# A position-bias table read in reversed query order, and softmax factors applied to the attention outputs

## The reference, cut to what matters

```python
def attend(qg, k, v):                                   # branch 1: grouped-query attention
    s = einsum('bqhgd,bkhd->bhgqk', qg, k) * ATTN_SCALE
    p = softmax(s, axis=-1)
    return einsum('bhgqk,bkhd->bqhgd', p, v)

# branch 2: neighbourhood attention on an 8 x 64 grid of tokens, window 8 rows x 16 columns
    s_win = einsum('bqhd,bwqjhd->bhqwj', q_row, k_win) * ATTN_SCALE
    row_bias_idx = r0 + arange(wr) - r + (NA_WIN_ROWS - 1)
    bias = rpb[:, row_bias_idx][:, :, col_bias_idx]      # rpb: 8 heads x 15 x 31
    s_win = s_win + bias
    s_ctx = einsum('bqhd,bkhd->bhqk', q_row, k_ctx) * ATTN_SCALE
    p = softmax(concatenate([s_win, s_ctx]), axis=-1)
    out = p_win @ v_win + p_ctx @ v_ctx
```

## Time and profile before

| | |
|---|---|
| median of 3 runs | 2911.68 us (2910.14 to 2912.68) |
| profiled execution, its own time | 2918.17 us |
| its span (first to last instruction) | 2916.4 us |
| mean granted TensorE clock | 0.95 |
| PE busy | 2612.7 us, 90% of the span |
| DVE busy | 1824.7 us, 63% |
| ACT busy | 1199.6 us, 41% |
| DMA | 435.32 MB, mean 149 GB/s |
| `normalise` (L2406, 64 times) | 39.8 us busy on DVE |

### The profile page before, as it was taken

How to read it: one execution, slowest core, us unless ns; L and a number is a source line. 1 busy time by engine, 2 the same in 40 slices (tenths; PEclk the granted TensorE clock), 3 DMA queues, 4 the chain that set the end, 5 groups by cost and what they waited for, 6 DMA issues and landing times.

```text
span 2916.4 us, 31985 instructions
## 1 busy us (share of the span) xinstructions
PE 2612.7 (90%) x11595; PEld 2012.7 (69%) x11595; DVE 1824.7 (63%) x2751; ACT 1199.6 (41%) x1698; POOL 150.9 (5%) x186
## 2 busy tenths in 40 slices
PE   5887889898888499999699979999999997999998
PEld 2675666565676387888575756888887575688886
DVE  5553477677676698999647765444443776544545
ACT  4321155444433277777443154323333315432232
POOL 0110000000000011111101100000000110000000
PEclk8897999999998699999799989999999998999999
DMA  6566524543442499999623342232223334222322
GB/s 223 155 192 188 182 87 111 133 117 89 147 162 84 152 376 362 371 365 354 209 93 113 95 123 72 87 101 89 98 91 101 105 104 121 65 87 101 101 86 79
DMA packets 237174, 435.32 MB, mean 149 GB/s; under 512 B 71264, under 2 KB 94048, under 8 KB 237055
## 3 DMA queue, kind: packets, MB, share of 16 engines
q1 hardware_dynamic: 219823, 390.75, 41.0%
q0 software_dynamic: 17232, 43.02, 4.4%
HBM read 398.86 MB, written 50.56 MB: 154 GB/s over the span
## 4 chain that ended last, share of the span: by engine, by line
PE 55%; DVE 12%; ACT 5%; DMA 4%; issue 3%; SPq 0%; POOL 0%; DVEq 0%; ACTq 0%; POOLq 0%
PE BKP L818 26%; PE BKP L840 4%; PE BKP L839 4%; PE BKP L838 4%; PE BKP L1317 2%; PE BKP L1320 2%; PE BKP L1319 2%; DVE WL L2856 2%; PE BKP L1129 1%; DVE G L2475 1%; DMA W<-in_w_expert_gu_dram 1%; ACT WH L1872 1%; DMA G<-in_w_expert_gu_dram 1%; DVE hL L2856 1%; PE SCP L1357 1%
## 5 line engine op out<-in xcount | busy, mean ns | idle before, releaser
L2111 DVE TENSOR_TENSOR WL<-W,WH 128x2048 fp32r<-128x2048 f32 x126 | 288.6, 2292 | 385.8 <-ACT WH L1478 382.9
L1478 ACT ACTIVATE WH<-W 128x2048 fp32r<-128x2048 f32 x126 | 241.0, 1913 | 662.1 <-PE BKP L818 306.0
L818 PE MATMUL BKP<-hH,WH 128*128 128x512 f32 x896 | 357.4, 399 | 24.2 <-DVE WL L2111 8.6
L818 PE MATMUL BKP<-hL,WH 128*128 128x512 f32 x896 | 352.2, 393 | 0.0
L818 PE MATMUL BKP<-hH,WL 128*128 128x512 f32 x896 | 352.1, 393 | 0.0
L818 PEld LDWEIGHTS BKP<-hH,WH 128*128 128x128 f32 x896 | 170.4, 190 | 72.6 <-issue 17.8
L818 PE MATMUL BKP<-WH,hH 128*128 128x512 f32 (+2 forms) x448 | 181.3, 405 | 22.3 <-DVE WL L2111 15.4
L840 PE MATMUL BKP<-WH,aL 128*128 128x512 f32 x512 | 199.2, 389 | 0.0
L838 PE MATMUL BKP<-WH,aH 128*128 128x512 f32 x512 | 199.2, 389 | 0.0
L839 PE MATMUL BKP<-WL,aH 128*128 128x512 f32 x512 | 199.2, 389 | 0.0
L818 PEld LDWEIGHTS BKP<-hL,WH 128*128 128x128 f32 x896 | 170.1, 190 | 36.4
(11 more groups left out here) (540 smaller groups left out, 5588.3 us busy)
## 6 DMA issues: line engine op xcount, KB each, us to landing
W<-in_w_expert_gu_dram SPq DMA_DIRECT2D x46, 1024.0 KB, 7.4
G<-in_w_expert_gu_dram SPq DMA_DIRECT2D x46, 1024.0 KB, 7.6
W<-in_w_in_dram SPq DMA_DIRECT2D x42, 1024.0 KB, 5.2
W<-in_w_up_dram SPq DMA_DIRECT2D x32, 1024.0 KB, 5.2
W<-in_w_down_dram SPq DMA_DIRECT2D x32, 1024.0 KB, 5.1
W<-in_w_expert_down_dram SPq DMA_DIRECT2D x24, 1024.0 KB, 6.6
G<-in_w_expert_down_dram SPq DMA_DIRECT2D x22, 1024.0 KB, 6.7
X<-in_w_mod_dram SPq DMA_DIRECT2D x16, 1024.0 KB, 5.9
```

The source lines that it names most:

```text
L818: mm = pe.matmul(BK[j][:, 0:cols], lt, rh, start=start and a == 0, stop=stop and a == len(q) - 1, skip_group_check=True)
L1478: act.activation(WH[s][:], W[s][:] if raw is None else raw, ACT.Copy).then_inc(sems["w_hi"], 1)
L2111: v.tensor_tensor(WL[s][:], W[s][:] if raw is None else raw, WH[s][:].bitcast(F32), ALU.subtract).then_inc(sems["w_lo"], 1)
```

## The change

The position-bias table is kept once: `rpb_d` becomes one row of 3832 values (48 zeros, the 3720 values, 64 zeros), filled by three small DMAs. The bias is read with a step of +1 value from one partition to the next, which gives the query columns in reversed order; so the second stage works on reversed queries within each tile of 128: ACT stores them reversed (`queries_reversed`), the mask is built reversed, and the transposes of the probabilities use a reversed identity (held in `CM`, loaded from a new table), which puts the order right again. `CM` is loaded with the causal mask anew in each layer of the second block (7 loads for 6).

In both stages `normalise` is gone. PE transposes the unnormalised exponentials as soon as ACT has made them. Row sums of both heads are gathered (`DENA`), DVE inverts four at a time (`RDA`), PE spreads the inverses over the 64 channels of each head by 8 small fp32 matmuls into `BK[1]` (`inverse_rows`), and DVE multiplies the two heads' joined output, 128 x 512, once (`put`). At n = 0 PE now does inverse rows, transposes and values first and the gate matmuls last. On DVE a step now waits for ACT's exponential before `top`, and the convolution taps stand ahead of `gate_lo`.

```diff
@@ SP
-            def rpb_row(h):
-                load(rpb_d[h * 15:(h + 1) * 15], RPB[h * 15:(h + 1) * 15, :].unsqueeze(1).to_broadcast([15, 64, WIN]),
-                     "rpb_stored")
-            load(CM[:], t["k_causal"], "tab_landed")
+            load(CM[:], t["k_reversed"], "tab_landed")
-            load(RPB[:, 48:79], t["na_rpb"][0].rearrange("h m c -> (h m) c"), "rpb_landed")
+            load(rpb_d[:, 0:RPAD], ZERO[:, 0:RPAD], "rpb_stored")
+            load(rpb_d[:, RPBS - 64:RPBS], ZERO, "rpb_stored")
+            load(rpb_d[:, RPAD:RPBS - 64], t["na_rpb"].rearrange("o h m c -> o (h m c)"), "rpb_stored")
...
-            rpb_row(0)
-            rpb_row(1)
...
-                    src = bass.AP(rpb_d.tensor, h * (15 * 64 * WIN) + ((1 - rr) * 64 * WIN + 63),
-                                  [[WIN - 1, 64], [64 * WIN, 14], [1, 64]])
-                    load(ES[s][rr * 64:(rr + 1) * 64, :, :], src, f"bias_landed{s}")
+                    src = bass.AP(rpb_d.tensor, h * (15 * WIN) + (1 - rr) * WIN, [[1, 64], [WIN, 14], [1, 64]])
+                    load(ES[s][(1 - rr) * 64:(2 - rr) * 64, :, :], src, f"bias_landed{s}")
@@ PE, attend
                 def turned(n):
-                    pe.wait_ge(sems["head_pn"], T.next("head_pn"))
+                    pe.wait_ge(sems["head_exp"], T.next("head_exp") if read == "head_nm" else T.at("head_exp", 0))
...
+                def inverse_rows():
+                    pe.wait_ge(sems["head_rd"], T.next("head_rd", 2))
+                    pe.wait_ge(sems["gt_ev"], T.at("gt_ev"))
+                    for tt in range(NT):
+                        for hd in range(2):
+                            mm = pe.matmul(BK[1][hd * HD:(hd + 1) * HD, tt * P:(tt + 1) * P],
+                                           RDA[:, hd, tt:tt + 1].to_broadcast([P, HD]), eye[:],
+                                           start=True, stop=True, skip_group_check=True)
+                    mm.then_inc(sems["inv_pe"], 1)
...
-                        if beside:
+                        if n == 0 and not first:
+                            inverse_rows()
+                            turned(n)
+                            values(1)
+                            pe.wait_ge(sems["inv_cp"], T.next("inv_cp"))
                             beside(n)
+                            continue
+                        beside(n)
                         turned(n)
@@ ACT
-            blk(copies(lambda j: ST[1][:, j, :], UN, 4, "st_filled1"))
+            def queries_reversed():
+                tiles = lambda ap: ap.rearrange("p (t q) -> p t q", t=NT)
+                for j in range(4):
+                    out(j)
+                    act.activation(tiles(ST[1][:, j, :]), tiles(BK[j])[:, :, ::-1], ACT.Copy).then_inc(sems[BANKS[j]], 1)
...
@@ DVE, attend
-                def normalise(n):
-                    c, nk = n % 2, keys(n % NT)
-                    v.wait_ge(sems["head_exp"], T.next("head_exp"))
-                    link(v.reciprocal(RD[:, c:c + 1], DEN[:, c:c + 1]))
-                    v.tensor_scalar(PR[c][:, 0:nk], PR[c][:, 0:nk], RD[:, c:c + 1], None, ALU.mult).then_inc(
-                        sems["head_pn"], 1)
+                def inverse(s):
+                    v.wait_ge(sems["head_exp"], T.at("head_exp"))
+                    v.reciprocal(RDA[:, s, :], DENA[:, s, :]).then_inc(sems["head_rd"], 1)
+                def factors_in(i):
+                    v.wait_ge(sems["inv_pe"], T.next("inv_pe"))
+                    link(v.tensor_copy(stage_of(i), BK[1]))
+                    v.sem_inc(sems["inv_cp"], 1)
+                def put(i):
+                    v.wait_ge(sems["head_o"], T.next("head_o", 2))
+                    v.tensor_tensor(stage_of(i), BK[0], stage_of(i), ALU.mult).then_inc(sems["head_y"], 1)
...
+                        if not (first and n == 0):
+                            v.wait_ge(sems["head_exp"], T.next("head_exp"))
                         if n + 1 < 2 * NT or not last:
                             top((n + 1) % (2 * NT), bias if n + 1 < 2 * NT else bias_next)
-                        normalise(n)
+                        if tt == NT - 1:
+                            inverse(s)
...
```

More of the change, by code:

```diff
@@ L45 @@
 BIG_E = 1.0e30
-WIN = 127
+WIN = 31
+RPAD = 48
+RPBS = RPAD + 8 * 15 * WIN + 64
 SLOTS = P
@@ L221, in program @@
         TINY = F[:, 1, 16:17]
+        DENA, RDA = (AF[:, r, :].rearrange("p (s t) -> p s t", s=2) for r in (3, 0))
         RDW = [AT[:, c:c + 256].rearrange("p (t s c) -> p t s c", t=2, s=2) for c in (512, 1280)]
@@ L485, in heads @@
                     T.skip("head_lo", 2)
-                    sp.wait_ge(sems["head_oe"], T.next("head_oe", 2))
+                    sp.wait_ge(sems["head_o"], T.next("head_o", 2))
                     sp.sem_inc(sems["paused"], 1)
@@ L495, in heads @@
                     for s in range(2):
[L496 removed]
+                        sp.wait_ge(sems["head_o"], T.next("head_o"))
                         sp.sem_inc(sems["paused"], 1)
@@ L657, in layer @@
                 sp.sem_inc(sems["paused"], 1)
+                load(CM[:], t["k_causal"], "lay_landed")
                 load(TC, t["k_retc"], "lay_landed")
@@ L1026, in gates, with attend @@
                     mm.then_inc(sems["side_mm"], 1)
-            def attend(count, loads, keys, PTB, read, beside=None):
+            def attend(count, loads, keys, PTB, read, eye, beside=None):
                 chunks = lambda n: range(0, keys(n % NT), 512)
@@ L1053, in turned, with values @@
                         for k0 in range(c0, min(c0 + 512, keys(n % NT)), P):
-                            mm = pe.transpose(TP[:, bank + k0 - c0:bank + k0 - c0 + P], PR[n % 2][:, k0:k0 + P], IDN[:])
+                            mm = pe.transpose(TP[:, bank + k0 - c0:bank + k0 - c0 + P], PR[n % 2][:, k0:k0 + P], eye[:])
                         mm.then_inc(sems["head_pt"], 1)
-                def values(s):
+                def values(s, free=True):
                     done = sum(len(chunks(tt)) for tt in range(NT))
                     pe.wait_ge(sems["head_ptc"], T.next("head_ptc:full", done))
-                    pe.wait_ge(sems["head_oe"], T.next("head_oe"))
+                    if s == 0 and free:
+                        pe.wait_ge(sems["head_y"], T.next("head_y"))
                     pe.wait_ge(sems[f"head_landed{s}"], T.next(f"head_landed{s}", 16 * loads))
@@ L1076, in body @@
                             T.skip(read)
-                        if beside:
+                        if n == 0 and not first:
[3 more added lines that the diff above has]
+                            pe.wait_ge(sems["inv_cp"], T.next("inv_cp"))
                             beside(n)
+                            continue
+                        beside(n)
                         turned(n)
-                        if n % NT == 0 and not (first and n == 0):
-                            values(1 if n == 0 else 0)
+                        if n == NT:
+                            values(0, not first)
                 for b in BANKS:
@@ L1092, in attend @@
                 body(False, True)
+                inverse_rows()
                 values(1)
                 T.skip("head_ptc:free", 2)
-                pe.wait_ge(sems["head_oe"], T.next("head_oe", 2))
-            attend(8, 1, lambda tt: KEYS, PTB_1, "head_exp", gates)
+                pe.wait_ge(sems["inv_cp"], T.next("inv_cp"))
+                pe.wait_ge(sems["head_y"], T.next("head_y"))
+            attend(8, 1, lambda tt: KEYS, PTB_1, "head_exp", IDN, gates)
             T.skip("head_nm", 8 * NT)
-            attend(8, 1, lambda tt: KEYS, PTB_1, "head_nm", gates)
-            T.skip("head_exp", 8 * NT)
+            attend(8, 1, lambda tt: KEYS, PTB_1, "head_nm", CM, gates)
             T.skip("side_used", 8)
@@ L2372, in conv_in, with attend @@
                 v.wait_ge(sems[BANKS[3]], T.at(BANKS[3]))
-            v.wait_ge(sems["rpb_stored"], T.at("rpb_stored", 16 * 8))
+            v.wait_ge(sems["rpb_stored"], T.at("rpb_stored", 16 * 3))
             link(v.memset(Z[:], 0.0))
             blk(conv_in, False)
-            def attend(count, keys, bias, put_out, load_incs, other=None, beside=None):
+            def attend(count, keys, bias, stage, load_incs, other=None, beside=None):
                 def remainders(s):
@@ L2479, in _ @@
                 gate_lo(0, q)
-            attend(8, lambda tt: KEYS, None, to_stage(1), 0, beside=conv_taps(0))
+            attend(8, lambda tt: KEYS, None, 1, 0, beside=conv_taps(0))
             def mixed_remainders(s, l):
```

68 lines of the change are left out of this document (30 added, 38 removed).

## The result

The changed kernel takes 2871.87 us in the median of 4 runs (2868.49 to 2874.49), the kernel before 2911.98 us in 4 runs on the same chip. The ratio is 0.9863, 95% interval 0.9845 to 0.9880: 40 us faster. I had forecast 2890 and a range of 2876 to 2905, so the sign was right and the size was not: the kernel gained nearly twice what I said.

A forecast was written before the change was run, and what follows sets the result against it. PE, busy 90% of the span, was taken to bound the kernel. Projections -27.9, normalise -12, inverse rows +16.8 and second block +1 sum to -22.1 us, from 2911.68 to 2889.6, forecast as 2890 us; range 2876 to 2905.

The forecast's parts named there:

- table (projections and second block): Projections: removing the bias stores closes two PE holes, -27.9 us; second block: one more small load per layer, +1 us.
- normalise out and factors in: Attention stages: multiplications leave DVE, -12 us; PE's small fp32 matmuls for the inverses come in, +16.8 us.
- the part on `normalise`: Attention: transposes no longer wait for DVE's multiplication; -12 us taken, bounds -14 and +2.
- wholly in series: Attention step: DVE plus ACT would take 6.8 us against PE's 6.3, losing 16 us in a stage.
- the wait list: PE's waits in the second attention stage: 11.0 us for `normalise`, 3.5 us of remainder waits inside the stage.
- Inverse rows: Both attention stages: 8 small fp32 matmuls on PE at each of 8 places, 2.1 us each, +16.8 us.
- the 1.3 us that I had named as a sign of being wrong: Attention: the prediction is wrong if `inverse_rows` takes under 1.3 us at a place, or over 3.
- rival 2: Inverse rows in attention: column halves overlap, so +7.6 us for 16.8, time 2880 us; chance 18%.
- Projections: Before attention: gains of 14.8, 2.6, 6.5 and 4.0 us from closed holes and full clock, -27.9 us in all.
- both holes: Projections: PE idles 15.39 us behind query stores and 6.55 us behind a late weight load; both delayed by bias stores.
- hole 1: Projections: PE idle 15.39 us up to 232.11, through ACT's wait for query stores; 14.8 us of it to be gained.
- Rivals 1, 3 and 4: 1: first hole closes by 5.9 us, 2901, 15%; 3: projections gain nothing, 2918, 4%; 4: slow bias reads, 2923, 4%.

The follow-up runs named there:

- e3: The kernel before with the table part alone (one row, reversed queries, mask and identity), normalise and the order of the taps kept: 2889.85 us, ratio 0.9927.
- e4: The kernel before with the table part and the taps ahead of `gate_lo`, normalise kept, no inverse rows: 2864.13 us, ratio 0.9839.
- e2: The changed kernel with `gate_lo` put back ahead of the taps, normalise still gone: 2897.53 us, ratio 0.9943 to the kernel before.
- e1: The kernel before with only the taps moved ahead of `gate_lo` in both attention stages, normalise kept: 2885.65 us, ratio 0.9909.
- e6: The changed kernel with inverse rows issued as four matmuls for one head, then four for the other: 2872.98 us, ratio 0.9861 to the kernel before.
- e5: The kernel before, unedited, profiled a second time: 2912.23 us.

## Why the prediction was wrong, step by step

| term, us | predicted | measured |
|---|---|---|
| table (projections and second block) | -27.9 + 1 | -22.2 (e3) |
| order of the taps | no term | -25.7 (e3 to e4, e2 to changed) |
| normalise out and factors in | -12 + 16.8 = +4.8 | +7.7 (e3 to e2, e4 to changed) |
| sum | -22.1 | -40.2; by the medians -40.1 |

- **The step that failed** is in the part on `normalise`: the taps in front of `gate_lo` stand in the words on the change, but got no term in the sum, which puts them at nothing without a reason. The runs give them 25.7 us. I even listed what is queued behind `top` and added busy times up to a step (6.8 us "wholly in series"), and then dismissed the series because "only `top` and the exponential are". In the trace rounding, `gate_lo` and the taps were in series too, 28.7 us of DVE's waits stood there over three pairs, and I had looked at PE's waits alone. I had also held the 6.8 against 6.3 us of PE a step, a mean that includes the 5.3 us of each head's values. A step without values takes PE 4.1 us, and the ring of 5.57 us is longer than that.
- **The credit went to the wrong edit.** The earlier trace rows says that transposes waited 11.0 us for L2406. That is true and is no price: L2406 was the last link that a late ring went through. e1 took those waits away and left the instruction in.
- **The size** of the wait list was too small as well: 21.5 us went from stage 2 in e1, where the list had 11.0 and 3.5 inside the stage.
- **Inverse rows**: the term was there, its size was off, because it left out that the halves overlap: 1.03 us for 2.1 a place, 8.2 us for 16.8. That is under the 1.3 us that I had named as a sign of being wrong. It is rival 2 for this term, close to its estimate of 0.95; the time that rival 2 gave, 2880 us, was missed as well, because of the taps. The Trainium skill's "TensorEngine Tiling (Array Packing)", section "Key Properties", says that tiles take weight loads and matmuls in parallel; the runs agree, 64 ns a record in alternating halves (changed kernel) for 94 in one half (e6). Its other sentence, that a change of tiling mode drains the array, costs little here: a pair grew by 1.2 us for the records' 1.03.
- **Projections**: both holes and their causes were right (ACT's wait for the query stores, SP held by the last pair), first scores at 340.9 for "near 343". But the wait did stay at 5.58 us, over nothing, and hid behind PE's work. Between the two profiled executions the first scores moved by 29.6 us, close to my 27.9. But that was the size of one execution, in which hole 1 was 15.4 us; in three others it was 9.2 to 9.6 in two parts, of which the second waited for a weight load. I then took the profiled execution's 6.5 us over the median off both kernels alike, though a good part of it seems to have been this very hole, which the change removes (first scores at 370.5 us for 365.6 in e5, whose time is that of the median). Some 5 us of the term were then never there in the median; that is worked out, not tested by a run.
- **Nothing hidden failed**: reversed queries are copied in 0.60 us an instruction as before, bias reads land in 6.1 us, and no wait for `BK[1]` or the exponential holds PE. Rivals 1, 3 and 4 did not occur.

The errors were of both signs: -25.7 missing, +8.6 too much on the inverse rows, some 5 too much gain in the projections, and some 11 of gain given to `normalise` that it does not have (its removal and the factors cost 7.7 us together, of which the inverse rows are 8.2).

## What to carry to other kernels

When an engine waits in turn with another, follow one step of the loop through both engines' rows from a result to the next of its kind; only what lies on that ring has a price, whichever instruction the wait list names. An order of independent work on an engine is an edit with a price of its own: put what needs nobody between giving work out and waiting for its return. And size a hole from more than one execution of the kernel before.

## What the runs showed of the hardware

- fp32 matmuls of a 64-wide stationary and 128 columns: 64 ns a record when column halves alternate (changed kernel), 94 ns in one half (e6). I had expected 114 to 137.
- The profile shows the same 202 matmul records as 45.72 us busy in a stream with stops (kernel before) and 43.90 without (e1).
- Eight DRAM writes of 960 pieces of 508 bytes each, 3.9 MB in all, cost PE 22 us (e3) through the loads and stores that queue beside and behind them, and from one execution to another the first hole that they make moved between 9.2 and 15.4 us.
